# Hybrid decoder block, forgetting attention: VectorE's side jobs issued behind the low parts of a step instead of ahead of them

## The chip, the cores and the metric

One core of a Trainium2 chip runs the whole program. The metric is the device time of one execution in microseconds (us), the median of several runs. Five engines matter: TensorE (PE: matrix products and transposes; PEld: its weight loads), VectorE (DVE), ScalarE (ACT), GpSimd (POOL, next to idle here) and SyncE (SP, which issues all transfers). Each engine works through its own instructions strictly in the order written; they meet at semaphores.

## The reference

One decoder block over 1024 tokens of width 1024, all in float32:

```
h = rms_norm(x);  proj = h @ w_in
qa, ka, va, fa, qb, kb, vb, ga, gb = split(proj)
log_f = log_sigmoid(fa + b_forget);  F = cumsum(log_f)
oa = softmax(qa ka^T / 8 + F_q - F_k, causal) @ va          # "forgetting" attention, 8 heads of 64
ob = mixture over 3 dilated sliding-window attentions        # 12 heads of 64, with rotary embedding
mixed = sigmoid(ga) * (oa @ w_branch_a) + sigmoid(gb) * (ob @ w_branch_b)
x = x + mixed @ w_out
x = x + relu(rms_norm(x) @ w_up)^2 @ w_down
return rms_norm(x)
```

## The kernel before, in words

**Precision.** TensorE is fed with fp32r operands. Every operand is split into a high part (a copy rounded to fp32r, made on ScalarE) and a low part (the rest, `operand - high`, made on VectorE), and a product is three matmuls: high x high, high x low, low x high. So each tensor needs a ScalarE copy and then a VectorE subtraction before TensorE may use it. The subtractions are the "low parts" and "splits" of this text.

**Stages.** The program first norms x, then runs ten attention *units* t = 0 to 9 of two heads each (`mixer_steps`): t = 0 to 5 are the dilated ones (`N_DIL` = 6), t = 6 to 9 the forgetting ones. Then come gates, branch products, output product and the MLP. Four `merge` jobs that sum the three dilated groups are done in the first two steps of t = 6.

**A unit** has 16 steps (G counts steps over all units, s = G mod 16 is the step in its unit). A step is one head and one tile of 128 queries. In a forgetting unit the queries are causal, so a step handles 1, 2, 1, 2, 3, 4, 3, 4, 5, 6, 5, 6, 7, 8, 7, 8 key tiles of 128 for s = 0 to 15. Steps of at least five tiles are worked in two pieces of at most four tiles ("units_of"), which take turns in the two halves of one PSUM tensor.

What the engines do in step G, in this order:

- TensorE: `scores(G)` (L1165), a third of a project part (L1122; the matrix products for the next units' keys, queries and values, which need the weight splits), `transposes(G-1)` of the probabilities (L1176), two more thirds of projection, and in odd steps `values` for an earlier pair of steps (L1197). In step 1 of a unit also the transposes of the values (L1206).
- VectorE: in even steps first `outs` (L2196: adds the two head halves; waits for ScalarE's `o_part`, which waits for TensorE's `values`); then `maxes(G)` (L2175: adds the bias, finds the row maximum; waits for the scores); then the first side job; then `probs_lo(G-1)` (L2182: the low part of the transposed probabilities); in even steps `query_lo` (L2156); in step 1 `values_lo` (L2163); then the other side jobs.
- ScalarE: `exps(G)` (L1627; waits for `maxes(G)`), then `probs_hi(G-1)` (L1637; the high part of the transposed probabilities), then its own splits (L1519, L1599). Before `exps` it has the evacuation of a finished projection (L1559) and `out_part` (L1652).

`transposes(G)` waits for `exps(G)`, and its piece n for the low part of piece n-2, since the pieces share two PSUM halves: in the steps of two pieces that is the low part of the step just before. `scores(G)` waits for `exps(G-2)`.

**Side jobs** of a step are listed by `side_work(G)`. In the forgetting units they are: a half of a weight chunk's low part, `split_lo` (L2077, 128x512; table `LO_STEPS`); a head's key low part, `k_stack` (L2148, 64x1024; table `K_LO_STEPS`); the normalising of the unit before, `normalise` (L2212, 128x1024, step 7); and in the first two steps of t = 6 the four merges (L2206, 128x1024). Nearly every step has one job or none. The steps with jobs are

| unit | split halves | key splits | normalise | merges |
|---|---|---|---|---|
| t = 6 | 2 (two), 6, 7, 13, 14 | 4, 5 | | 0 (two), 1 (two) |
| t = 7 | 3, 4, 9, 10, 14, 15 | 11, 12 | 7 | |
| t = 8 | 5, 6, 12, 13 | 9, 10 | 7 | |
| t = 9 | 3, 4, 10 (two) | | 7 | |

SyncE's loads of later weight chunks wait for the splits too (`w_lo`), with at least a chunk of lead.

Of the kernel before, what the change touches and what calls it, by code (L numbers as in the profile page):

```python
# [53 lines left out]
N_DIL = 2 * len(DILATIONS)  # L54
# [235 lines left out]
def build(nc, x, g_attn, w_in, b_forget, w_branch, w_out, g_mlp, w_up, w_down, g_final, rope, f_rows, r_rows, x_mid, hidden, sg, out):  # L290
# [8 lines left out]
    with ExitStack() as ctx:  # L299
# [1763 lines left out]
        def _(dve):  # L2063
# [19 lines left out]
            for half in range(2):  # L2083
# [7 lines left out]
                for i in range(4):  # L2091
                    t = 4 * half + i
# [58 lines left out]
            def query_lo(B):  # L2151
                t, b = divmod(B, BLOCKS)
                row = 64 * (b % 2)
                cols = slice(b // 2 * 2 * P, (b // 2 + 1) * 2 * P)
                dve.wait_ge(q_hi, 2 * B + 1)
                dve.scalar_tensor_tensor(out=q_st(B)[row:row + 64, 1, :], in0=q_raw(t)[row:row + 64, cols], scalar=-QSCALE,  # L2156
                                         in1=q_st(B)[row:row + 64, 0, :].bitcast(F32),
                                         op0=ALU.mult, op1=ALU.subtract).then_inc(q_lo, 1)

            def values_lo(t):  # L2160
                for bank in range(2):
                    dve.wait_ge(v_hi, 2 * t + bank + 1)
                    dve.tensor_tensor(v_part[1][:, 4 * bank:4 * bank + 4, :, :],  # L2163
                                      PS[2][:, bank * HALF:(bank + 1) * HALF].rearrange("p (t h d) -> p t h d", t=4, h=2),
                                      v_part[0][:, 4 * bank:4 * bank + 4, :, :].bitcast(F32),
                                      ALU.subtract).then_inc(v_lo, 1)

            def maxes(G):
                n = len(tiles_of(G))
                dve.wait_ge(qk_done, G + 1)  # L2170
                if G >= STEPS * N_DIL and G % STEPS == 0:
                    f = G // STEPS - N_DIL
                    dve.wait_ge(fbias_in[f % 2], 32 * (f // 2 + 1))
                sc = psc[G % 2][:, 0:n * P]
                dve.tensor_tensor_reduce(sc, sc, score_bias(G, n), 1.0, FMAX, ALU.add, ALU.min,  # L2175
                                         stat(G, 0)).then_inc(max_done, 1)

            def probs_lo(G):
                for n, (a, b) in enumerate(units_of(G)):
                    u = units_before(G) + n  # L2180
                    dve.wait_ge(pt_hi, u + 1)
                    dve.tensor_tensor(pt_tiles(G, 1, a, b),  # L2182
                                      PS[2][:, (u % 2) * HALF:(u % 2) * HALF + (b - a) * P].rearrange("p (j c) -> p j c", c=P),
                                      pt_tiles(G, 0, a, b).bitcast(F32), ALU.subtract).then_inc(pt_lo, 1)

            def inverses(f):
                dve.wait_ge(exp_done, STEPS * (N_DIL + f + 1))
                cols = slice(f * STEPS, (f + 1) * STEPS)
                dve.reciprocal(rowinv[:, cols], fox_stat[:, 1, cols]).then_inc(inv_done, 1)

            def outs(B):
                t, b = divmod(B, BLOCKS)
                row = 64 * (b % 2)
                dst = og[:, t // 2, (t % 2) * 1024:(t % 2 + 1) * 1024] if t < N_DIL else keep[:, (t - N_DIL) * 1024:(t - N_DIL + 1) * 1024]
                dve.wait_ge(op_done, B + 1)
                dve.tensor_tensor(pair_tokens(dst[row:row + 64], t, b // 2), pair_view(o_bank(B)[row:row + 64, :], t),  # L2196
                                  pair_view(o_part[row:row + 64, :], t), ALU.add).then_inc(on_done, 1)
# [16 lines left out]
            def side_work(G):  # L2214

                t, s = divmod(G, STEPS)
                u = t + 1
                jobs = []
                if t == MIX - 1 and s == 10:
                    jobs += [lambda: split_lo(CH0 + 3 * t + 5, 0), lambda: split_lo(CH0 + 3 * t + 5, 1)]  # L2220
                if t < N_DIL:
                    for s0, s1, c in ((3, 4, 3 * t + 4), (8, 8, 3 * t + 5), (14, 14, 3 * t + 6)):
                        jobs += [lambda c=c: split_lo(CH0 + c, 0)] if s == s0 else []
                        jobs += [lambda c=c: split_lo(CH0 + c, 1)] if s == s1 else []
                    if s in (9, 15):
                        jobs.append(lambda: k_stack(u, (s - 9) // 6))
                elif (t, s) in LO_STEPS:
                    jobs.append(lambda: split_lo(CH0 + LO_STEPS[t, s][0], LO_STEPS[t, s][1]))
                if s in K_LO_STEPS.get(t, ()):
                    jobs.append(lambda: k_stack(u, K_LO_STEPS[t].index(s)))  # L2230
                if t == N_DIL and s in (0, 1):
                    jobs += [lambda: merge(2 * s), lambda: merge(2 * s + 1)]
                if t == N_DIL and s == 2:
                    jobs += [lambda: split_lo(CH0 + 23, 0), lambda: split_lo(CH0 + 23, 1)]
                if t > N_DIL and s == 7:
                    jobs.append(lambda: normalise(t - N_DIL - 1))
                if u < N_DIL:
                    jobs += [lambda n=n: rotate(u, n // 8, n // 4 % 2, n % 4) for n in ROTATE_OPS.get(s, ())]
                return jobs

            def mixer_steps(first, last):
                for G in range(first, last + 3):
                    t, s = divmod(G, STEPS)
                    if G % 2 == 0 and first <= G - 4 < last:
                        outs((G - 4) // 2)
                    jobs = side_work(G) if G < last else []
                    if G < last:
                        maxes(G)
                    for job in jobs[:1]:
                        job()  # L2250
                    if first <= G - 1 < last:
                        probs_lo(G - 1)
                        if first and G > first and s == 0:
                            inverses(t - N_DIL - 1)
                    if G < last and G % 2 == 0 and G // 2 + 1 < BLOCKS * MIX:
                        query_lo(G // 2 + 1)
                    if s == 1 and G < last:
                        values_lo(t)
                    for job in jobs[1:]:
                        job()  # L2260

            for n in range(8):
# [6 lines left out]
            split_lo(4)  # L2269
            query_lo(0)  # L2270
            mixer_steps(0, STEPS * N_DIL)


# [26 lines left out]
            for n in range(6):  # L2300
                g, pair = divmod(n, 2)
                dve.wait_ge(spr_done, n + 1)
                own = og[:, g, pair * 1024:(pair + 1) * 1024]
                dve.tensor_tensor(own, PS[pair][:], own, ALU.mult).then_inc(spr_out, 1)
            mixer_steps(STEPS * N_DIL, STEPS * MIX)


# [528 lines left out]
```

## Time and profile before

| what | value |
|---|---|
| median of 3 runs | 1602.18 us (1600.99 to 1605.12) |
| the profiled execution: own time | 1602.5 us |
| its span in the trace | 1600.7 us |
| PE busy | 1517.0 us (95%), PEld 1243.0 (78%) |
| DVE busy | 1100.1 us (69%) |
| ACT busy | 784.1 us (49%) |
| forgetting units (t = 6 to 9) | about 384.7 to 631 us of the span |

The profiled execution takes 1.8 us more than its span, which lies around the first and last instruction. Starts are in us from the span's start. A group's idle time is that of the engine just before its instructions; behind the arrow stands what ended it. A PE that is busy in this count is not always at its peak, since its matmuls overlap.

### The profile page before, as it was taken

What the parts mean: (1) busy time and instruction counts of PE and PEld (TensorE: products, weight loads), DVE (VectorE), ACT (ScalarE), POOL (GpSimd) and SP (SyncE); (2) the same over time, 40 slices, a digit from 0 to 9 for tenths busy, and PEclk for the clock granted to TensorE, in tenths of its full rate; (3) what the DMA queues carried; (4) which work ended last, traced back from release to release, by engine and by line L of the source; (5) the groups of instructions that cost most, each with busy time, mean ns of one, the idle gap of its engine ahead of it and who ended that gap; (6) DMA issues with size and microseconds to landing.
All of it is one profiled execution on the core that took longest, in us unless ns stands there. A gap on an engine that the chain in (4) does not pass through costs nothing. (4 is left out here: it accounts for less than half of the span.)

```text
span 1600.7 us, 20827 instructions
## 1 busy us (share of the span) xinstructions
PE 1517.0 (95%) x7364; PEld 1243.0 (78%) x7364; DVE 1100.1 (69%) x1749; ACT 784.1 (49%) x1436; POOL 4.8 (0%) x22
## 2 busy tenths in 40 slices
PE   6999999998999998999999989999999899999997
PEld 5787777776777877788888878888888677777776
DVE  4677777755666666943675676766667787777776
ACT  5566666663666665534224454343334444444441
POOL 1000000000000000000000000000000000000000
PEclk9999999999999999999999999999999999999998
DMA  5321111111022111333655333444444774444402
GB/s 184 93 65 29 41 53 41 27 40 27 14 67 65 29 41 34 105 118 100 194 174 152 99 92 124 159 150 161 162 154 169 248 264 145 145 145 145 145 27 106
DMA packets 168277, 173.40 MB, mean 108 GB/s; under 512 B 7848, under 2 KB 127720, under 8 KB 167792
## 3 DMA queue, kind: packets, MB, share of 16 engines
q1 hardware_dynamic: 168176, 172.07, 33.5%
q8 instruction: 61, 1.00, 0.3%
q14 instruction: 40, 0.33, 0.1%
HBM read 125.84 MB, written 46.20 MB: 107 GB/s over the span
## 5 line engine op out<-in xcount | busy, mean ns | idle before, releaser
L1122 PE MATMUL ps<-hspl,wsp 128*128 128x512 f32 x1536 | 423.3, 408 | 8.8 <-ACT tmp L1559 5.1
L1122 PEld LDWEIGHTS ps<-hspl,wsp 128*128 128x128 f32 x1536 | 265.2, 190 | 55.5 <-ACT tmp L1559 7.3
L1474 PE MATMUL ps<-dn_b,a_hi 128*128 128x512 f32 x896 | 279.1, 393 | 17.1 <-DVE keep L2309 11.4
L1474 PEld LDWEIGHTS ps<-dn_b,a_hi 128*128 128x128 f32 x896 | 167.3, 189 | 59.5 <-issue 21.7
L1474 PE MATMUL ps<-dn_b,a_lo 128*128 128x512 f32 x448 | 175.2, 391 | 0.0
L2309 DVE TENSOR_TENSOR keep<-keep,ps 128x512 f32<-128x512 f32 (+1 forms) x144 | 101.4, 712 | 42.7 <-PE ps L1474 24.3
L1474 PE MATMUL ps<-up_b,a_hi 128*128 128x512 f32 x384 | 119.6, 393 | 4.9 <-ACT keep L1908 3.8
L2182 DVE TENSOR_TENSOR work<-ps,work 128x128 fp32r<-128x128 f32 (+3 forms) x144 | 59.1, 420 | 65.8 <-ACT work L1637 63.7
L1932 ACT ACTIVATE keep<-keep 128x512 f32<-128x512 f32 x64 | 40.5, 633 | 126.0 <-DVE keep L2611 42.0
L1474 PEld LDWEIGHTS ps<-dn_b,a_lo 128*128 128x128 f32 x448 | 84.4, 188 | 17.9
L1176 PE MATMUL ps<-ident,tmp 128*128 128x128 f32 x428 | 74.7, 276 | 21.1 <-issue 8.0
L2309 DVE TENSOR_TENSOR dn_b<-dn_raw,dn_b 128x1024 fp32r<-128x1024 f32 x56 | 67.1, 1221 | 39.4 <-ACT dn_b L1948 39.3
L1176 PEld LDWEIGHTS ps<-ident,tmp 128*128 128x128 f32 x428 | 52.1, 140 | 48.8 <-issue 27.0
L2475 DVE TENSOR_TENSOR a_lo<-a_raw,a_hi 128x1024 fp32r<-128x1024 f32 (+1 forms) x66 | 81.3, 1234 | 11.0 <-ACT a_hi L1898 10.9
L1474 PEld LDWEIGHTS ps<-up_b,a_hi 128*128 128x128 f32 x384 | 72.6, 190 | 20.6 <-issue 4.0
L1908 ACT COPY ps<-ps 128x512 f32<-128x512 f32 x46 | 26.3, 571 | 122.6 <-PE ps L1474 115.8
L1627 ACT ACTIVATE tmp<-ps,fox_stat 128x128 f32<-128x128 f32 (+3 forms) x64 | 47.5, 743 | 72.4 <-DVE fox_stat L2175 72.3
L1474 PE MATMUL ps<-up_t,a_hi 128*128 128x512 f32 x256 | 78.9, 389 | 0.0
L1474 PE MATMUL ps<-up_t4b,a_hi 128*128 128x512 f32 x256 | 78.8, 389 | 0.0
L1627 ACT ACTIVATE tmp<-ps,dil_stat 128x128 f32<-128x128 f32 (+1 forms) x96 | 40.1, 417 | 73.8 <-DVE dil_stat L2175 73.6
L1474 PE MATMUL ps<-up_b,a_lo 128*128 128x512 f32 x192 | 75.3, 392 | 0.0
L1197 PEld LDWEIGHTS ps<-work 128*128 128x128 f32 x456 | 68.3, 190 | 7.3 <-DVE work L2182 1.6
(240 smaller groups left out, 2827.1 us busy)
## 6 DMA issues: line engine op xcount, KB each, us to landing
hidden<-keep SPq DMA_DIRECT2D x112, 256.0 KB, 2.2
dn_raw<-hidden SPq DMA_DIRECT2D x56, 512.0 KB, 6.1
raw<-in_w_in SPq DMA_DIRECT2D x35, 512.0 KB, 3.8
a_raw<-in_w_up SPq DMA_DIRECT2D x36, 256.0 KB, 3.1
sgl<-sg SPq DMA_DIRECT2D x8, 1024.0 KB, 5.1
a_raw<-in_w_down SPq DMA_DIRECT2D x32, 256.0 KB, 3.0
spare<-in_w_down SPq DMA_DIRECT2D x32, 256.0 KB, 3.7
spare<-in_w_up SPq DMA_DIRECT2D x28, 256.0 KB, 3.2
```

Of the source, the lines that this page charges most:

```text
L1122: ins = pe.matmul(psp(u, g), wsp[c % 2][:, wp, k * P:(k + 1) * P], hspl[:, mp, k, cols], start=(n == 0), stop=(n == 23), skip_group_check= ...
L1176: ins = pe.transpose(PS[2][:, (u % 2) * HALF + (k - a) * P:(u % 2) * HALF + (k - a + 1) * P], probs(G)[:, k * P:(k + 1) * P], ident[:])
L1197: ins = pe.matmul(o[:, cols], v_nat[:, j, 2 * (b % 2):2 * (b % 2) + 2, :].rearrange("p a d -> p (a d)"), moving, start=(part == 0 and (n = ...
L1474: ins = pe.matmul(o, a_part(n, j, wp, k), b_block(n, j, mp, k), start=(first and k == 0 and m == 0), stop=(k == ks - 1 and m == 2), skip_g ...
L1627: act.activation(probs(G)[:, 0:n * P], psc[G % 2][:, 0:n * P], ACT.Exp, bias=stat(G, 0), scale=-1.0, accum_out=stat(G, 1)).then_inc(exp_do ...
L1908: act.copy(s1[q] if q < 2 else bank_b(q), bank_a(q)).then_inc(s1_ok, 1)
L1932: act.activation(u, u, ACT.Square).then_inc(signal, 1)
L2182: dve.tensor_tensor(pt_tiles(G, 1, a, b), PS[2][:, (u % 2) * HALF:(u % 2) * HALF + (b - a) * P].rearrange("p (j c) -> p j c", c=P), pt_til ...
L2309: return dve.tensor_tensor(out, a, b, op)
L2475: dve.tensor_tensor(a_lo_t[q % 2][b][:], src[:], a_hi_t[q % 2][b][:].bitcast(F32), ALU.subtract).then_inc(a_lo, 1)
```

## The change

In steps of the forgetting units (t at least `N_DIL`) the first side job is no longer issued between `maxes(G)` and `probs_lo(G-1)`; all side jobs are issued behind `probs_lo`, `query_lo` and `values_lo`, at the end of the step. The dilated units stay as they were. No instruction is added, removed or resized; TensorE's, ScalarE's, GpSimd's and SyncE's orders are as before.

```diff
                     jobs = side_work(G) if G < last else []
                     if G < last:
                         maxes(G)
-                    for job in jobs[:1]:
+                    early = 1 if t < N_DIL else 0
+                    for job in jobs[:early]:
                         job()
                     if first <= G - 1 < last:
                         probs_lo(G - 1)
...
                     if s == 1 and G < last:
                         values_lo(t)
-                    for job in jobs[1:]:
+                    for job in jobs[early:]:
                         job()
```

VectorE in t = 6, steps 4 and 5 (L2175: maxes and its accumulator read, L2148: key split, L2182: low part of the probabilities, L2156: query, L2196: outs):

```order
 L2175 ISA ps,fox_stat<-ps,fbias_57 128x384
 L2175 ISA fox_stat 128x1
-L2148 TENSOR_TENSOR work<-tmp,work 64x1024
 L2182 TENSOR_TENSOR work<-ps,pt_odd 128x2x128
 L2156 SCALAR_TENSOR_TENSOR q_fox<-tmp,q_fox 64x256
+L2148 TENSOR_TENSOR work<-tmp,work 64x1024
 L2175 ISA ps,fox_stat<-ps,fbias_57 128x512
 L2175 ISA fox_stat 128x1
-L2148 TENSOR_TENSOR work<-tmp,work 64x1024
 L2182 TENSOR_TENSOR work<-ps,work 128x3x128
+L2148 TENSOR_TENSOR work<-tmp,work 64x1024
 L2196 TENSOR_TENSOR keep<-ps,o_part 64x256
```

Both key splits moved from ahead of the low part to the step's end: that of step 4 now stands directly ahead of the next maxes, that of step 5 ahead of the outs.

VectorE in t = 6, steps 13 and 14 (L2077: half of a weight chunk's split):

```order
-L2077 TENSOR_TENSOR wsp_54<-raw_52,wsp_54 128x512
 L2182 TENSOR_TENSOR work<-ps,work 128x4x128
 L2182 TENSOR_TENSOR work<-ps,work 128x3x128
+L2077 TENSOR_TENSOR wsp_54<-raw_52,wsp_54 128x512
 L2196 TENSOR_TENSOR keep<-ps,o_part 64x256
 L2175 ISA ps,fox_stat<-ps,fbias_57 128x896
 L2175 ISA fox_stat 128x1
-L2077 TENSOR_TENSOR wsp_54<-raw_52,wsp_54 128x512
 L2182 TENSOR_TENSOR work<-ps,work 128x4x128 x2
 L2156 SCALAR_TENSOR_TENSOR q_fox<-tmp,q_fox 64x256
+L2077 TENSOR_TENSOR wsp_54<-raw_52,wsp_54 128x512
```

The split half of step 13 moved behind the two low pieces and stands ahead of outs and the next maxes; that of step 14 moved behind low pieces and query.

## Rows read from the trace of the kernel before

**Rows 1.** The page's busy times of each engine over the span.

```profile
PE 1517.0 (95%) x7364; PEld 1243.0 (78%) x7364; DVE 1100.1 (69%) x1749; ACT 784.1 (49%) x1436; POOL 4.8 (0%) x22
```

**Rows 2.** Groups by line, 384 to 631 us: busy, mean ns, idle before, releaser.

```profile
L1627 ACT ACTIVATE tmp<-ps,fox_stat 128x128 f32<-128x128 f32 (+3 forms) x64 | 47.5, 743 | 72.4 <-DVE fox_stat L2175 72.3
L1176 PE MATMUL ps<-ident,tmp 128*128 128x128 f32 x288 | 43.0, 275 | 11.4 <-DVE work L2182 7.7 <-issue 3.4
L2182 DVE TENSOR_TENSOR work<-ps,pt_odd 128x512 fp32r<-128x512 f32 (+3 forms) x48 | 25.3, 555 | 31.4 <-ACT pt_odd L1637 31.1
...
L2077 DVE TENSOR_TENSOR wsp<-raw,wsp 128x512 fp32r<-128x512 f32 x20 | 13.7, 683 | 0.0
...
L2148 DVE TENSOR_TENSOR work<-tmp,work 64x1024 fp32r<-64x1024 f32 x6 | 7.3, 1220 | 0.2
...
L2212 DVE TENSOR_TENSOR keep<-keep,tmp 128x1024 f32<-128x1024 f32 x3 | 3.7, 1218 | 0.4 <-DMA tmp<-r_rows 0.4
```

**Rows 3.** Timeline: t = 9 step 13; t = 6 step 13 (VectorE); t = 9 steps 10, 11.

```profile
613.42 1.23 DVE L2175 CUSTOM_DVE_ANT_0 ps<-ps,fbias 128x1024 f32<-128x1024 f32 x1
...
614.79 1.12 ACT L1627 ACTIVATE tmp<-ps,fox_stat 128x1024 f32<-128x1024 f32 x1 [2.20 <-DVE fox_stat L2175]
...
615.90 0.96 ACT L1637 CAST work<-ps 128x512 fp32r<-128x512 f32 x2
616.51 1.15 DVE L2182 TENSOR_TENSOR work<-ps,work 128x512 fp32r<-128x512 f32 x2 [1.75 <-ACT work L1637]
...
433.48 0.69 DVE L2077 TENSOR_TENSOR wsp<-raw,wsp 128x512 fp32r<-128x512 f32 x1
435.31 1.16 DVE L2182 TENSOR_TENSOR work<-ps,work 128x512 fp32r<-128x512 f32 x2 [1.15 <-ACT work L1637]
...
604.60 0.68 DVE L2077 TENSOR_TENSOR wsp<-raw,wsp 128x512 fp32r<-128x512 f32 x1
...
605.20 0.95 DVE L2175 CUSTOM_DVE_ANT_0 ps<-ps,fbias 128x768 f32<-128x768 f32 x1
```

**Rows 4.** Timeline, VectorE, t = 6 step 4: key split, then low part.

```profile
399.90 1.22 DVE L2148 TENSOR_TENSOR work<-tmp,work 64x1024 fp32r<-64x1024 f32 x1
401.15 0.42 DVE L2182 TENSOR_TENSOR work<-ps,pt_odd 128x256 fp32r<-128x256 f32 x1
```

**Rows 5.** Waits (us in total, times, longest) in 384:448, 448:507, 507:565, 565:631 in turn.

```profile
DVE keep L2196 <- ACT o_part L1652: 3.9, 3, 1.6
DVE work L2163 <- ACT work L1619: 1.4, 1, 1.4
...
DVE keep L2196 <- ACT o_part L1652: 3.2, 6, 0.8
DVE work L2163 <- ACT work L1619: 2.8, 1, 2.8
...
DVE keep L2196 <- ACT o_part L1652: 3.4, 5, 1.0
...
DVE keep L2196 <- ACT o_part L1652: 1.4, 3, 0.6
DVE work L2163 <- ACT work L1619: 1.6, 1, 1.6
```

**Rows 6.** Timeline, TensorE: waits in t = 6 steps 3 and 15, t = 7 step 15.

```profile
395.88 0.71 PE L1122 MATMUL ps<-hspl,wsp 128*128 128x512 f32 x2 [1.48 <-DVE wsp L2077]
...
440.64 1.05 PE L1176 MATMUL ps<-ident,tmp 128*128 128x128 f32 x7 [0.99 <-DVE work L2182]
...
502.07 1.05 PE L1176 MATMUL ps<-ident,tmp 128*128 128x128 f32 x7 [1.52 <-DVE work L2182]
```

**Rows 7.** Timeline, t = 7: low part of step 12, and the transposes of step 13.

```profile
496.21 1.16 DVE L2182 TENSOR_TENSOR work<-ps,work 128x512 fp32r<-128x512 f32 x2 [1.75 <-ACT work L1637]
...
497.05 1.06 PE L1176 MATMUL ps<-ident,tmp 128*128 128x128 f32 x8
```

## The prediction

> **What bounds the kernel now.** I read the page's busy times first, then the groups and the waits of the forgetting units alone, then the timeline of single steps. Over the span TensorE is the fullest engine at 95%, VectorE has 69% [rows 1]. That average hides what happens in the four units that the change touches. There ScalarE sits idle 72.4 us before its exps, 72.3 of it until VectorE's maxes are done, and VectorE sits idle 31.4 us before the low parts of one buffer (about as long before those of the other), until ScalarE's high parts are done [rows 2]. The two engines feed each other in a ring: maxes(G), exps(G), high part(G-1), low part(G-1), and behind the low part the next maxes. One turn, in t = 9 step 13 [rows 3]: maxes start at 613.42, exps at 614.79, the high part at 615.90, the low part at 616.51, and VectorE has done nothing for 1.75 us before it. TensorE is close behind: its transposes sit idle 7.7 us in all until a low part is done [rows 2], with single waits of 0.99 and 1.52 us late in a unit [rows 6], but it has no such waits in most of the smaller steps. So two chains of nearly equal length run side by side: the ring, and TensorE's own work. Where TensorE is the later one, VectorE waits for it at outs (3.9, 3.2, 3.4 and 1.4 us in the four units) and once a unit at the values' low part (1.4, 2.8, 2.8, 1.6; the row of 2.8 stands for t = 7 and, word for word again, for t = 8) [rows 5].
>
> **What the old place costs.** Nothing in nearly every step. The job stands in the gap in which VectorE waits for ScalarE: with a split half in t = 6 step 13 the job starts at 433.48, and the low part still waits 1.15 us more at 435.31, until the high part [rows 3]. The reader should see that the job only shortens the idle time. A key split of 1.22 us is longer than some gaps of small steps: in t = 6 step 4 the low part follows it with no idle time [rows 4]; a step of that size without so long a job reaches its low part some 1.05 us behind its maxes, so 0.2 us is all the job costs there.
>
> **What the new place costs.** Behind the low part there is no such gap: the next is maxes (after an even step) or outs (after an odd one), and maxes do not wait for TensorE. The ring gets longer by the job, less the idle time that VectorE has at outs. Prices: a split half 0.60 us, from start to start of the next in the one place where a half already stands there (604.60 to 605.20) [rows 3], against a duration of 0.68; a key split 1.25 from start to start [rows 4]; normalise 1.22 [rows 2], of which I count 1.15. The gap itself does not shrink, since ScalarE still needs it, so the job's old time comes back as idle time.
>
> Now unit by unit, as the lag that each unit adds to TensorE, since TensorE's lag is what cannot be taken back at outs:
>
> - t = 6. Step 0 only swaps a merge and the query: 0. Step 1: a merge (128x1024 like normalise, 1.22 long [rows 2], counted 1.14 from start to start) moves behind the values' low part, which gets 0.16 earlier: +0.98. Step 2: a half, +0.60, and TensorE already waits 1.48 us for just this split [rows 6], so 1.58 goes straight to TensorE. Steps 4 to 7: 1.05 + 1.25 + 0.60 + 0.60 = 3.50, less the 1.20 us (one of the three waits that make the 3.9 [rows 5]; the others are 1.55 and 1.11) that VectorE waits at outs of step 6; the 1.55 ahead of step 4 give nothing, as both are late alike. The transposes around step 11 start only 0.2 us behind what they wait for, so TensorE has taken over about 2.1 of these 2.30 by the next outs wait. Step 13: +0.60, less 0.1. Step 14 falls under the values' wait of the next unit (2.8) [rows 5]. Unit: 1.58 + 2.07 + 0.50 = 4.15.
> - t = 7. Steps 3, 4, 9, 10 halves (2.4), 7 normalise (1.15), 11 and 12 key splits (2.5): 6.05 by step 13. Outs waits up to there: 3.2 [rows 5] less the last one of 0.56 = 2.62. Left 3.43, and no time for TensorE to hide it: the transposes of step 13 start at 497.05, and the first piece of the low part of step 12 (0.69 of the 1.16 from 496.21) is done at 496.9 [rows 7], 0.1 earlier; the next ones wait 1.52 us already [rows 6]. Unit: 3.33. Steps 14 and 15 fall under the next values' wait.
> - t = 8. Halves in 5, 6, 12, 13 (2.4), normalise 1.2, key splits in 9 and 10 (2.5): 6.1. Outs waits 3.4 [rows 5] less the 1.03 of step 4, ahead of the first job: 2.37. Unit: 3.73 less 0.1 = 3.6.
> - t = 9. Halves in 3 and 4 (1.2), normalise 0.83 (it waited 0.44 us for a transfer and held the low part up, which is won back), the first half of step 10 (0.6): 2.63. Of the outs waits of 1.4 [rows 5] count 0.59, 0.16 and 0.1 of the third, TensorE being late by then, less 0.1: 1.7.
>
> Sum: 4.15 + 3.33 + 3.6 + 1.7 = **12.8 us**. Dilated units and everything behind t = 9 are unchanged. Loads and the splits themselves end 1 to 4 us later but are wanted a step or more later, except in t = 6 step 3, counted. The profiled execution took 1602.5 us, so 1615.3; it lies 0.3 above the median, so I expect **1615.0 us** as the median.
>
> **Bounds of the unknown.** How much TensorE's own reserve takes up no row tells directly. If nothing absorbed anything, all moved jobs count in full: 6.28 + 7.25 + 6.1 + 2.63 = 22.3 us. If in each unit all of VectorE's waits for TensorE, at outs and at the values, were free for the jobs, the units cost 6.28 - 5.3 = 1.0, 7.25 - 6.0 = 1.25, 6.1 - 6.2 and 2.63 - 3.0, so 0: 2.2 us. I take the middle value since rows 6 and 7 show TensorE with 0.1 us or nothing in hand exactly where the lag has piled up.
>
> **The rivals.**
>
> *TensorE covers it.* TensorE is the bound of a whole unit, and the ring catches up at each values' low part. For it: 95% busy, and 2.8 us of VectorE's waits there in t = 7 and 8 [rows 1, 5]. Against it: TensorE's waits of 0.99 and 1.52 us on low parts late in the unit [rows 6], through which a late ring is handed on before the catching-up point. Time: 1602.2 + 2.2 = 1604.4. Beside this stands the Trainium skill, "Perfetto Trace Analysis", section "Identifying the Most-Contended Engine": the engine with the highest occupancy is the most contended and the one to work on. By that rule an order on an engine of 69% would be worth nothing while TensorE stands at 95%, and the time would be 1602.2; the waits between engines speak against it here.
>
> *Full exposure.* The outs waits do not absorb, because TensorE gets late at once. For it: transposes follow exps closely in some steps. Against it: in early steps TensorE shows no waits at all. Time: 1602.2 + 22.3 = 1624.5.
>
> *Faster.* The low parts come earlier, so TensorE's transposes stop waiting. It decides if the jobs, and not ScalarE, release the low parts. The price is the 7.7 us of TensorE's waits on low parts [rows 2]: 1594.5. Against it: VectorE is idle before nearly all low parts, with a job or without [rows 3]; the low part that is held up is held by 0.2 us [rows 4]. Without that mechanism what is left of it is under 1 us.
>
> *Another thing than told:* the moved jobs could make a step's scores or loads late. All have a step or more in hand; it would add to the forecast, not replace it.
>
> **How the numbers follow.** A difference under 0.3% (4.8 us) counts as no change here. My forecast (12.8, with 8 to 18 as its own range) gets 0.70, TensorE covering it (up to 4.8) 0.16, full exposure 0.11, faster 0.03. Slower by over 4.8 us holds the first and third: 0.81; no change 0.16; faster 0.03. The range of 8 in 10 leaves out the coverer and the far end of full exposure: 1607 to 1622.
>
> **What would show it.** In the changed profile: no side job between maxes and low part in t = 6 to 9; idle time before low parts up by about the 20 us of the moved jobs (31.4 and its twin, together some 62, towards 80); each of the units t = 6 to 8 longer by 3 to 4 us, t = 9 by 2; VectorE's waits at outs smaller than in rows 5; more TensorE idle before transposes, by about 10 us over the 7.7. The units before t = 6 and all after t = 9 the same length. I am wrong if the four units together grow by under 5 us (TensorE had reserve), or if the idle time before the low parts does not grow (the jobs were not hidden before).

## The result and the profile after

| | kernel before | changed kernel |
|---|---|---|
| median | 1601.59 us (1600.80 to 1605.12, 4 runs) | 1620.23 us (1618.33 to 1620.52, 4 runs) |
| the profiled execution: span | 1600.7 us | 1616.5 us |
| 0 to the first maxes of t = 6 | 384.7 us | 384.7 us |
| from there to the last maxes of t = 9 | 237.5 us | 253.6 us |

The ratio of the medians is 1.0100, 95% interval [1.0084, 1.0116]: the change costs 1.0%, by the medians 18.6 us, by the profiled executions 15.8 us. The units themselves grow by 16.1 us; the 2.5 us more of the medians have no place in the two traces, where all that stands behind the last maxes took 978.5 and 978.2 us. Over the twelve traces of this text that last part took 977.6 to 984.5 us, so medians and spans carry a few us that the units do not explain, and the growth of the units is the sharper instrument here.

The page's busy times stand beside [rows 1]:

```profile
PE 1520.8 (94%) x7364; PEld 1244.5 (77%) x7364; DVE 1099.7 (68%) x1749; ACT 783.9 (48%) x1436; POOL 4.8 (0%) x22
```

VectorE and ScalarE did the same work in the same time. Only TensorE's busy time grew, by 3.8 us (2.6 of them in the four units), which the order of another engine's jobs should not do; about 1.6 of these 2.6 us are a slow clock, taken up below. Where the time lies the busy times by stretch tell (us; then busy time and instructions of PE, PEld, DVE, ACT and POOL; granted clock, DMA share, GB/s):

```profile
0.00:384.00 384.00, 355.03 (x1876) 288.66 (x1877) 262.65 (x629) 228.16 (x579) 4.83 (x22) 1.00 0.20 61
384.00:647.00 263.00, 229.81 (x1353) 187.04 (x1353) 159.02 (x332) 154.61 (x361) 0.00 (x0) 0.99 0.12 35
647.00:1616.00 969.00, 935.95 (x4137) 768.84 (x4136) 678.08 (x789) 401.13 (x496) 0.00 (x0) 0.99 0.44 145
```

The same work took 247 us before (384 to 631), and the rest is as long as it was. All of the loss is in the four forgetting units. The groups there, to hold against [rows 2]:

```profile
L1122 PE MATMUL ps<-hspl,wsp 128*128 128x512 f32 x456 | 137.1, 420 | 13.0 <-ACT tmp L1559 9.7 <-DVE wsp L2077 3.2
L1627 ACT ACTIVATE tmp<-ps,fox_stat 128x128 f32<-128x128 f32 (+3 forms) x64 | 47.5, 742 | 89.2 <-DVE fox_stat L2175 89.1
L1176 PE MATMUL ps<-ident,tmp 128*128 128x128 f32 x288 | 43.3, 276 | 17.3 <-DVE work L2182 12.8 <-issue 3.4 <-ACT tmp L1627 0.9
L2182 DVE TENSOR_TENSOR work<-ps,pt_odd 128x512 fp32r<-128x512 f32 (+3 forms) x48 | 25.3, 555 | 42.1 <-ACT pt_odd L1637 42.1
L2182 DVE TENSOR_TENSOR work<-ps,work 128x512 fp32r<-128x512 f32 (+3 forms) x48 | 25.3, 555 | 41.5 <-ACT work L1637 41.5
```

- ScalarE waits 89.1 us for maxes instead of 72.3: +16.8, about the whole loss. The maxes come late, and with them the exps.
- VectorE waits 83.6 us in front of the low parts instead of some 62: +22. The jobs that filled the gap are gone from it, and the gap is as long as before.
- TensorE waits 12.8 us for low parts at its transposes (7.7 before), 3.2 for a weight split (1.5 before) and 9.7 for ScalarE's evacuation of a finished projection. That last one was 3.9 in the kernel before, a row I had not read.

The waits of VectorE at outs in the four units (384 to 451, 451 to 515, 515 to 579, 579 to 647 us), and the one at the values' low part that changed, in t = 8, to hold against [rows 5]:

```profile
DVE keep L2196 <- ACT o_part L1652: 4.2, 2, 3.1
...
DVE keep L2196 <- ACT o_part L1652: 1.1, 3, 0.6
...
DVE keep L2196 <- ACT o_part L1652: 1.2, 2, 1.0
DVE work L2163 <- ACT work L1619: 2.4, 1, 2.4
...
DVE keep L2196 <- ACT o_part L1652: 0.8, 2, 0.6
```

The outs waits fell in t = 7 to 9 (3.2, 3.4, 1.4 before), as forecast, and did not fall in t = 6. There one single wait of 3.07 us stands at step 4:

```profile
402.11 0.42 DVE L2196 TENSOR_TENSOR keep<-ps,o_part 64x256 f32<-64x256 f32 x1 [3.07 <-ACT o_part L1652]
```

It was 1.55 before, of the 3.9 of [rows 5]; the wait of 1.20 at step 6 is gone, taken up by late jobs as forecast. Something slowed TensorE between 394 and 402 us. The wait for the weight split is part of it; the rest is the clock, as the next timeline shows. It is TensorE from step 3 of t = 6 on, first after, then before:

```profile
397.54 0.71 PE L1122 MATMUL ps<-hspl,wsp 128*128 128x512 f32 x2 [3.21 <-DVE wsp L2077]
...
398.12 2.80 PE L1122 MATMUL ps<-hspl,wsp 128*128 128x512 f32 x6
400.72 0.95 PE L1197 MATMUL ps<-work 128*128 128x256 f32 x4
```

```profile
396.45 1.62 PE L1122 MATMUL ps<-hspl,wsp 128*128 128x512 f32 x6
397.91 0.57 PE L1197 MATMUL ps<-work 128*128 128x256 f32 x4
```

The same six matmuls take 2.80 us instead of 1.62, and the next four 0.95 instead of 0.57. The granted clock of these microseconds (the eighth figure, behind POOL's) is full before the wait and half behind it:

```profile
398.00:399.00 1.00, 1.00 (x5) 0.73 (x3) 0.25 (x1) 0.95 (x4) 0.00 (x0) 0.62 0.39 58
399.00:400.00 1.00, 1.00 (x4) 0.80 (x3) 0.04 (x1) 0.65 (x1) 0.00 (x0) 0.50 1.03 300
400.00:401.00 1.00, 1.00 (x5) 0.81 (x4) 0.00 (x0) 0.00 (x0) 0.00 (x0) 0.50 0.56 166
401.00:402.00 1.00, 1.00 (x7) 0.84 (x7) 0.00 (x0) 0.29 (x1) 0.00 (x0) 0.67 0.00 0
402.00:403.00 1.00, 1.00 (x7) 0.84 (x7) 0.89 (x3) 0.49 (x2) 0.00 (x0) 1.00 0.00 0
```

In the kernel before, the clock is 1.00 all through this stretch. So TensorE ran at 1.2 GHz in place of 2.4 for some 3 us, right behind a wait of 3.21 us. From the two matmul groups it costs (2.80 - 1.62) + (0.95 - 0.57) = 1.56 us.

### The profile page after: what moved, and what is told of

Same layout as the page of the kernel before. It is cut to its first block and busy times, and to the rows that moved or that the text cites. A ratio compares the mean times of both kernels' runs of the same rounds, so it can differ in the third digit from the quotient of the medians.

```text
span 1616.5 us, 20827 instructions
## 1 busy us (share of the span) xinstructions
PE 1520.8 (94%) x7364; PEld 1244.5 (77%) x7364; DVE 1099.7 (68%) x1749; ACT 783.9 (48%) x1436; POOL 4.8 (0%) x22
## 5 line engine op out<-in xcount | busy, mean ns | idle before, releaser
L1474 PE MATMUL ps<-dn_b,a_hi 128*128 128x512 f32 x896 | 279.8, 394 | 16.6 <-DVE keep L2310 12.1
L1474 PEld LDWEIGHTS ps<-dn_b,a_hi 128*128 128x128 f32 x896 | 167.5, 189 | 59.1 <-issue 22.8
L1474 PE MATMUL ps<-dn_b,a_lo 128*128 128x512 f32 x448 | 175.5, 392 | 0.0
L1474 PE MATMUL ps<-up_b,a_hi 128*128 128x512 f32 x384 | 120.2, 395 | 4.8 <-ACT keep L1908 3.8
L2182 DVE TENSOR_TENSOR work<-ps,work 128x128 fp32r<-128x128 f32 (+3 forms) x144 | 59.1, 420 | 76.9 <-ACT work L1637 74.7
L1176 PE MATMUL ps<-ident,tmp 128*128 128x128 f32 x428 | 74.9, 276 | 27.1 <-DVE work L2182 12.8
L1474 PEld LDWEIGHTS ps<-dn_b,a_lo 128*128 128x128 f32 x448 | 84.8, 189 | 17.9
L1627 ACT ACTIVATE tmp<-ps,fox_stat 128x128 f32<-128x128 f32 (+3 forms) x64 | 47.5, 742 | 89.2 <-DVE fox_stat L2175 89.1
L1474 PEld LDWEIGHTS ps<-up_b,a_hi 128*128 128x128 f32 x384 | 73.0, 191 | 20.6 <-issue 4.0
L1474 PE MATMUL ps<-up_t4b,a_hi 128*128 128x512 f32 x256 | 79.5, 392 | 0.0
L1474 PE MATMUL ps<-up_t,a_hi 128*128 128x512 f32 x256 | 78.9, 389 | 0.0
L1474 PE MATMUL ps<-up_b,a_lo 128*128 128x512 f32 x192 | 75.6, 394 | 0.0
L1197 PEld LDWEIGHTS ps<-work 128*128 128x128 f32 x456 | 68.7, 191 | 7.4 <-DVE work L2182 1.6
```

The source lines that it names most:

```text
L1176: ins = pe.transpose(PS[2][:, (u % 2) * HALF + (k - a) * P:(u % 2) * HALF + (k - a + 1) * P], probs(G)[:, k * P:(k + 1) * P], ident[:])
L1197: ins = pe.matmul(o[:, cols], v_nat[:, j, 2 * (b % 2):2 * (b % 2) + 2, :].rearrange("p a d -> p (a d)"), moving, start=(part == 0 and (n = ...
L1474: ins = pe.matmul(o, a_part(n, j, wp, k), b_block(n, j, mp, k), start=(first and k == 0 and m == 0), stop=(k == ks - 1 and m == 2), skip_g ...
L1627: act.activation(probs(G)[:, 0:n * P], psc[G % 2][:, 0:n * P], ACT.Exp, bias=stat(G, 0), scale=-1.0, accum_out=stat(G, 1)).then_inc(exp_do ...
L2182: dve.tensor_tensor(pt_tiles(G, 1, a, b), PS[2][:, (u % 2) * HALF:(u % 2) * HALF + (b - a) * P].rearrange("p (j c) -> p j c", c=P), pt_til ...
```

## Where the lag comes in

I matched all 64 maxes of the units in the two traces and read the difference of their starts. How much each unit grows, in us (from the first maxes of t = 6 to those of t = 7 step 0, t = 8 step 2, t = 9 step 2 and t = 9 step 15), for the changed kernel and for the experiments below:

| kernel | t = 6 | t = 7 | t = 8 | t = 9 | sum |
|---|---|---|---|---|---|
| forecast | 4.15 | 3.33 | 3.6 | 1.7 | 12.8 |
| changed kernel | 6.4 | 4.0 | 3.6 | 2.1 | 16.1 |
| e1_not_first | 3.2 | 4.0 | 3.6 | 2.8 | 13.6 |
| e2_first_only | 2.9 | 0.0 | 0.0 | 0.2 | 3.1 |
| e3_odd_only | 2.2 | 1.2 | 1.2 | 0.7 | 5.3 |
| e4_even_only | 2.7 | 1.9 | 1.5 | 3.1 | 9.3 |
| h1_extra_early | 0.0 | 0.0 | 0.0 | 0.2 | 0.2 |
| h3_extra_late | 2.4 | 0.7 | 1.3 | 0.6 | 5.0 |
| f1_query_early | -2.1 | -0.9 | -0.9 | -1.5 | -5.4 |
| f3_query_outs_early | -3.4 | -1.8 | -1.4 | -3.9 | -10.4 |
| f4_order_late | 1.2 | 0.2 | -0.5 | -2.7 | -1.7 |

From here on "units" with a number means the last column. Each row is one traced execution. The spans grow by up to 6.3 us more than these sums (in f1; 4.9 in e3, 4.0 in f4, about 2 or less in the others): up to 1.2 us of that lies before t = 6 and the rest behind t = 9. The step of one split half is 0.58 to 0.61 us, very regular, in every step in which nothing takes it back.

## The experiments

### One part of the change at a time

The first two cut the change at the start of t = 6. e1 leaves steps 0 to 2 of t = 6 as they were, and e2 changes these three alone. The edit of e1:

```diff
-                    early = 1 if t < N_DIL else 0
+                    early = 1 if t < N_DIL or G < STEPS * N_DIL + 3 else 0
```

> Jobs moved as in the change except in steps 0 to 2 of t = 6, which stay as in the kernel before. Theory A (the moved jobs lengthen the ring of VectorE and ScalarE; VectorE's waits at outs absorb part): the span grows by 11 to 13 us over the kernel before, and the granted clock stays at full speed around 398 us. Theory B (every moved job costs in full, nothing absorbs): 21 us. Theory C (the loss is mostly the clock that fell after TensorE's long wait for the first split): only some 5 us.

Measured: 1616.08 us (1614.99 to 1616.77) against 1602.09, ratio 1.0088 [1.0074, 1.0101]; units +13.6, a little above the 11 to 13 expected. Some 0.7 us of it is one more wait, of 0.87 us, in which the normalise of t = 9, now at the step's end, waits for its transfer (0.15 us in the changed kernel). TensorE's wait for the split is 1.5 us again, and the clock stays full:

```profile
396.00:399.00 3.00, 2.07 (x10) 1.69 (x11) 1.48 (x5) 2.07 (x5) 0.00 (x0) 1.00 0.32 74
399.00:402.00 3.00, 3.00 (x19) 2.46 (x18) 1.01 (x4) 1.82 (x7) 0.00 (x0) 1.00 0.33 101
```

The edit of e2:

```diff
-                    early = 1 if t < N_DIL else 0
+                    early = 0 if STEPS * N_DIL <= G < STEPS * N_DIL + 3 else 1
```

> Only steps 0 to 2 of t = 6 changed (two merges and one split half moved). Theory A: the ring is 1.6 us late at maxes of step 3, TensorE's wait for the split grows from 1.5 to 3.2 us, the granted clock falls behind it as in the changed kernel and adds 1.5: 3.1 us in all, kept to the end. Rival (the clock's fall has another cause, such as a transfer at that time): 1.6 us and full clock. Theory C: 10 us or more.

Measured: 1605.01 us (1604.12 to 1607.66), ratio 1.0019 [1.0010, 1.0029]; units +3.1, of which t = 6 has 2.9. The wait and the slow clock are there with these three steps alone:

```profile
PE ps L1122 <- DVE wsp L2077: 3.2, 1, 3.2
```

```profile
400.00:401.00 1.00, 1.00 (x4) 0.81 (x3) 0.00 (x0) 0.33 (x1) 0.00 (x0) 0.50 1.13 343
401.00:402.00 1.00, 1.00 (x6) 0.91 (x6) 0.00 (x0) 0.00 (x0) 0.00 (x0) 0.50 0.18 52
402.00:403.00 1.00, 1.00 (x5) 0.66 (x5) 0.50 (x2) 0.79 (x2) 0.00 (x0) 0.65 0.00 0
```

So the first three steps cost their 1.6 us of late jobs and about 1.3 us of clock more, as expected, and everything else of the change costs 13.6 without the clock. 3.1 + 13.6 = 16.7, against the 16.1 of the whole; the rest is e1's longer wait for the transfer.

The expectation of e2 names a rival for the clock, a transfer at that time. There is one: DMA share 1.03 to 1.13 in the slow microseconds. But the same burst stands at full clock in other traces, as here in e4, where TensorE's wait for the split is 2.1 us:

```profile
399.00:400.00 1.00, 1.00 (x8) 0.85 (x7) 0.00 (x0) 0.46 (x2) 0.00 (x0) 1.00 1.14 346
```

So the transfer alone does not do it.

The next two cut it by kind of step. After an odd step an outs stands behind the moved job and may take it in; after an even one the maxes stand there. e3 moves the jobs of odd steps alone, e4 those of even steps alone. The edit of e3 (e4 has `s % 2 == 0`):

```diff
-                    early = 1 if t < N_DIL else 0
+                    early = 0 if t >= N_DIL and s % 2 else 1
```

> Jobs moved in odd steps alone (there outs, which waits for TensorE in many steps, stands behind the job). Theory A: 13.3 us of jobs are moved, the outs waits absorb more than half: some 5 us. Theory B: 13 us.

Measured: 1610.00 us (1609.07 to 1612.66), ratio 1.0054 [1.0042, 1.0067]; units +5.3, as expected. The median is up by 7.9; in the trace 1.0 us more lies before the units and 3.8 behind them.

> Jobs moved in even steps alone (there the next maxes stand behind the job, which wait for nothing but VectorE). Theory A: 8.6 to 9.8 us of jobs are moved; the next outs waits still absorb part, so some 5 us, and no fall of the clock. Theory B: 9 us. If odd and even together give much less than the change (under 11 against 16), the waits at outs are a reserve that is used up: each half alone fits into it, both together do not.

Measured: 1612.31 us (1610.26 to 1615.09), ratio 1.0068 [1.0055, 1.0081]; units +9.3. That is a miss, about 4 us over. Two of them come in at one place, t = 9 step 8, with the normalise job. It stands early in e4, as in the kernel before, and waits for its transfer:

```profile
600.35 1.23 DVE L2212 TENSOR_TENSOR keep<-keep,tmp 128x1024 f32<-128x1024 f32 x1 [2.45 <-DMA tmp<-r_rows]
```

It waited 0.44 us before. The transfer's load was issued at 595.47, behind the store of the inverse rows at 591.84 and a weight load at 591.43, in the order of SyncE's queue; before, the same three came at 586.45, 582.91 and 582.50, some 9 us earlier, while the maxes of step 7 lie only 7.4 us later than before. By the code the weight load waits for a split, which stands later in its step here, and the store stands behind that load in the queue; that this is the reason was not tried by itself. A job in the gap costs nothing only as long as what it waits for has come. In the whole change the normalise stands at the step's end and 0.15 us of this wait are left.

With the prices of the prediction the jobs of odd steps are 12.9 us long in all (t = 6: 3.6, t = 7: 4.2, t = 8: 3.65, t = 9: 1.4) and those of even steps 9.5. So 5.3 of 12.9 us show in odd steps, 41%, and 9.3 - 2.0 = 7.3 of 9.5 in even ones, 77%: the outs behind an odd step do take in a good part, and a job straight ahead of the maxes shows for the most part. The two halves without the 2 us sum to 12.6, the whole change without its clock to 16.1 - 1.5 = 14.6; so some 2 us of reserve are shared between them, far from the case (under 11 against 16) in which the expectation would have seen a reserve used up.

### Is the gap free, and is the end of the step what costs

The change moves 29 jobs of three sizes. A cleaner test adds one: a subtraction of 128x512 elements that writes to unused scratch memory and leaves the output as it is, in the 16 steps whose only split job is one half (the table's split halves without step 2 of t = 6 and step 10 of t = 9, which have two). h1 puts it in the gap, right behind the first side job, so that the gap must hold two:

```diff
+            def filler():
+
+                dve.wait_ge(dchain, chain[0])
+                chain[0] += 1
+                dve.tensor_tensor(stage5[:, :], hspl[:, 0, 0, 0:HALF].bitcast(F32), hspl[:, 1, 0, 0:HALF].bitcast(F32),
+                                  ALU.subtract).then_inc(dchain, 1)
...
                     for job in jobs[:1]:
                         job()
+                    if G < last and (t, s) in LO_STEPS:
+                        filler()
```

> The kernel before with one more subtraction of the size of a split half (128x512, read from SBUF, written to a scratch) in each of the 16 steps of LO_STEPS, in the gap between maxes and low part. Theory A (the gap is ScalarE's time and free for VectorE): the gap left there is 0.45 to 1.2 us against 0.6 us of work, so the four units grow by under 1 us. Rival (any work on VectorE costs, wherever it stands): 16 x 0.6 = 10 us.

Measured: 1602.95 us (1599.63 to 1605.99) against 1603.31, ratio 1.0000 [0.9990, 1.0010]; units +0.2 for 16 x 0.6 = 9.6 us of new work. The maxes of t = 7 step 0, t = 8 step 0 and t = 9 step 7 lie 1.14, 1.12 and 1.16 us behind those of the kernel before, and the first maxes of t = 6, ahead of all fillers, already 1.13. t = 6 step 13 on VectorE, to hold against the second part of [rows 3] (L2182 is the maxes' line in this kernel, L2189 that of the low part):

```profile
434.62 0.69 DVE L2077 TENSOR_TENSOR wsp<-raw,wsp 128x512 fp32r<-128x512 f32 x1
435.23 0.69 DVE L2172 TENSOR_TENSOR stage<-hspl 128x512 f32<-128x512 f32 x1
436.46 0.69 DVE L2189 TENSOR_TENSOR work<-ps,work 128x512 fp32r<-128x512 f32 x1 [0.55 <-ACT work L1637]
```

The low part comes 1.84 us behind the split, as before (433.48 to 435.31: 1.83), and its wait fell from 1.15 to 0.55. h3 has the same filler, behind `for job in jobs[1:]` at the step's end:

```diff
                     for job in jobs[1:]:
                         job()
+                    if G < last and (t, s) in LO_STEPS:
+                        filler()
```

> The same 16 additional subtractions, but at the end of their steps; the real jobs stay in the gap. Theory A: the units grow by what the change showed for the same steps, step by step together some 6.4 us (0.6 in most even steps, 0 in those odd steps that stand before a long wait at outs). If it is as little as in the run with the work in the gap, the place is not what costs.

Measured: 1608.51 us (1604.09 to 1612.22), ratio 1.0037 [1.0026, 1.0047]; units +5.0, so half of the 9.6 us, where some 6.4 were expected. The groups of h1, then of h3, in the four units:

```profile
L1627 ACT ACTIVATE tmp<-ps,fox_stat 128x128 f32<-128x128 f32 (+3 forms) x64 | 47.5, 742 | 72.8 <-DVE fox_stat L2182 72.7
L2203 DVE TENSOR_TENSOR keep<-ps,o_part 64x256 f32<-64x256 f32 x31 | 13.1, 421 | 12.4 <-ACT o_part L1652 11.7
```

```profile
L1627 ACT ACTIVATE tmp<-ps,fox_stat 128x128 f32<-128x128 f32 (+3 forms) x64 | 47.5, 743 | 79.3 <-DVE fox_stat L2182 79.2
L2203 DVE TENSOR_TENSOR keep<-ps,o_part 64x256 f32<-64x256 f32 x31 | 13.1, 421 | 9.2 <-ACT o_part L1652 8.6
```

In the gap the filler changes neither row (72.3 and 11.8 us in the kernel before); what it takes is VectorE's idle time before the low parts, 61.5 us before, 52.1 in h1 and again 61.5 in h3. At the step's end it lets ScalarE wait 6.5 us more for maxes. In VectorE's time, h3 against h1, the 9.6 us are 4.8 of longer units, 3.1 less of outs waits, 0.4 less at the values' low part and 0.7 less at the normalise's transfer; 0.6 stay unplaced.

### Turning it round: more work into the gap

If the ring bounds these units, whatever leaves its path should win time. In the forgetting units f1 puts the query's low part, which stood between the low part and the next maxes, ahead of the low part, into the gap:

```diff
+                    if t >= N_DIL and G < last and G % 2 == 0 and G // 2 + 1 < BLOCKS * MIX:
+                        query_lo(G // 2 + 1)
                     if first <= G - 1 < last:
                         probs_lo(G - 1)
...
-                    if G < last and G % 2 == 0 and G // 2 + 1 < BLOCKS * MIX:
+                    if t < N_DIL and G < last and G % 2 == 0 and G // 2 + 1 < BLOCKS * MIX:
                         query_lo(G // 2 + 1)
```

> The kernel before, with query_lo in the forgetting units ahead of the low part of the probabilities instead of behind it. Theory A read the other way round: 0.35 to 0.45 us leave the ring in each even step, where TensorE is not the bound: the units shrink by 1 to 4 us. Rival (TensorE's own work bounds the units): no change.

Measured: 1598.74 us (1595.57 to 1603.43) against 1603.31, ratio 0.9972 [0.9963, 0.9982]; units -5.4, more than the 1 to 4 expected. f3 has this edit and one more: outs no longer stands ahead of the maxes but behind them.

```diff
-                    if G % 2 == 0 and first <= G - 4 < last:
+                    if (not first or G >= last) and G % 2 == 0 and first <= G - 4 < last:
                         outs((G - 4) // 2)
                     jobs = side_work(G) if G < last else []
                     if G < last:
                         maxes(G)
+                    if first and G < last and G % 2 == 0 and first <= G - 4:
+                        outs((G - 4) // 2)
```

> As before, and outs also behind maxes, in the gap, instead of ahead of maxes, so that VectorE's wait for TensorE's values falls into the gap. Theory A: ring shorter by some 0.8 us in each even step; TensorE's waits on low parts (7.7 us) and on evacuations (3.9 us) are the most that can be won: 3 to 8 us faster. Rival: no change.

Measured: 1593.61 us (1591.88 to 1594.23), ratio 0.9942 [0.9930, 0.9954]; units -10.4, more than the 3 to 8 expected. This is faster than both kernels. Its groups in the units:

```profile
L1627 ACT ACTIVATE tmp<-ps,fox_stat 128x128 f32<-128x128 f32 (+3 forms) x64 | 47.5, 742 | 53.9 <-DVE fox_stat L2175 53.2
L1176 PE MATMUL ps<-ident,tmp 128*128 128x128 f32 x288 | 42.9, 275 | 5.2 <-issue 3.4 <-DVE work L2182 1.6
L2175 DVE CUSTOM_DVE_ANT_0 ps<-ps,fbias 128x128 f32<-128x128 f32 (+3 forms) x64 | 48.7, 762 | 20.2 <-PE ps L1165 19.8
```

ScalarE's waits for maxes fell by 19 us, and TensorE hardly waits for low parts now. The third row is new: VectorE waits 19.8 us for TensorE's scores in front of the maxes (1.2 us of idle time in all before). The ring has overtaken TensorE in many steps and TensorE is what bounds there.

### Both together

f4 is f3 with the change on top, f5 the kernel of f3 once more as its partner on the same chip.

> Query and outs early, as in f3_query_outs_early, and the change with it: the first side job of each step of t = 6 to 9 behind the low part. Theory A (the jobs cost because they lengthen the ring of VectorE and ScalarE, whatever else stands in it): the ring is shorter by the query and by the outs now, but the gap in front of the low part has no more idle time to give, and no outs wait is left that could take a job in. So the step from f3 to f4 should be no smaller than the 15.8 us of the change itself, up to the 22 us of all jobs in full where the ring is what bounds, and less by what the shorter ring leaves as TensorE's lead. I expect units t = 6 to 9 longer by 12 to 18 us than those of f3, so 1606 to 1612 us. Theory B (the gap is what costs, and a ring shortened by the new order has room for the jobs at its end): under 6 us more than f3, so below 1600.

> The kernel of f3_query_outs_early once more, on the same chip as f4, as its partner. Both theories: 8 to 10 us faster than the kernel before, ratio 0.994 to 0.995, as the first time.

Measured: f5 1593.11 us (1591.41 to 1593.87), ratio 0.9943 [0.9929, 0.9956], as the first time. f4 1602.79 us (1599.97 to 1605.86), ratio 1.0006 [0.9996, 1.0015]. So late jobs cost 9.7 us on this order by the medians, in the units 10.4 - 1.7 = 8.7 us, some 1.4 of them in the step of the slow clock again. Neither theory's figure came out: it is less than the 12 us or more that A asked for and more than the 6 that B allowed. The rows of f4 say why:

```profile
L2175 DVE CUSTOM_DVE_ANT_0 ps<-ps,fbias 128x128 f32<-128x128 f32 (+3 forms) x64 | 48.7, 761 | 11.7 <-PE ps L1165 11.2
L2182 DVE TENSOR_TENSOR work<-ps,pt_odd 128x512 fp32r<-128x512 f32 (+3 forms) x48 | 25.3, 555 | 31.3 <-ACT pt_odd L1637 31.3
```

Of f3's 19.8 us of waits for scores, 11.2 are left; 8.6 us of late jobs went into them for nothing. VectorE's waits for ScalarE before the low parts rose from 41.2 to 60.0 us, by 18.8 and not by the 22 us of all moved jobs, so part of the jobs seems to have cost time already in f3's fuller gap. I had written that the gap had nothing more to give and had overlooked that the ring itself now had reserve. By unit the change costs 4.6, 2.0, 0.9 and 1.1 here, in t = 8 a quarter of the 3.6 that it costs in the order before. What the change costs depends on which of the two chains is the later one, and by how much.

## Why the prediction was right, and where its sum was off

The median is 1620.2 us, forecast 1615.0 in 1607 to 1622, and the case that I held likeliest is the one that came. It lies 5.2 us over the forecast and near the upper end of the range: 3.3 us are misses in the units, taken apart below, and the rest is the few us of the medians that no trace places. That the range held them all is partly luck, since it had no term for the clock. By its own steps:

- **The gap is free, the step's end is not.** Right, and shown: 9.6 us of new work in the gap cost 0.2 us in the units (h1), at the step's end 5.0 (h3). Idle time before the low parts rose from 62 to 83.6 us, forecast "towards 80".
- **The prices.** A split half 0.60 from start to start: measured 0.58 to 0.61 in a dozen steps. Right.
- **The middle of the units.** Up to t = 6 step 13 the forecast has 1.58 + 2.07 us, measured are 1.54 (steps 2 and 3) and 2.07 (steps 5 to 8), apart from what step 4 brings. Up to t = 7 step 14: 3.40, forecast 3.33. t = 8: 3.6, forecast 3.6. t = 9: 2.1, forecast 1.7, its normalise step having brought 0.97 instead of 0.83. Right.
- **t = 6 step 4, missing.** "1.58 goes straight to TensorE" was right, and made TensorE's wait of [rows 6] 3.21 instead of 1.48 us; I did not ask what a wait of that length does to TensorE's clock. It fell to half, and the lag grew by 1.53 us in this one step. e1 (without them) and e2 (with them alone) show that it belongs to the first three steps; why the clock fell behind this wait is not shown (last section).
- **The last half of a unit, the step of the sum that was wrong.** "Step 14 falls under the values' wait of the next unit", and the same of steps 14 and 15 of t = 7. It did not: t = 6 grew by 0.58 and 0.59 in steps 14 and 15, where 0.50 in all was forecast, and nothing came back in t = 7; t = 7 grew by another 0.6 net. The values' wait of t = 7 is 2.8 us as before, that of t = 8 fell only to 2.4. TensorE had become as late by then. I had looked only at its transposes; it also waits for ScalarE's evacuation of a projection (L1559), and ScalarE does that in order, behind exps that are late with the maxes. In t = 7 step 0 the lag of the last half crosses over there, whole; TensorE before, then after:

```profile
445.26 0.73 PE L1122 MATMUL ps<-hspl,wsp 128*128 128x512 f32 x2 [0.50 <-ACT tmp L1559]
```

```profile
451.68 0.73 PE L1122 MATMUL ps<-hspl,wsp 128*128 128x512 f32 x2 [1.11 <-ACT tmp L1559]
```

The wait grew by 0.61 us, one half. The miss of 16.1 - 12.8 = 3.3 us is thus 1.5 of clock, 0.6 + 0.6 of last halves, 0.4 in t = 9 and 0.2 of small differences.

- **"More TensorE idle before transposes, by about 10 us":** it was 5.1 us on low parts, 5.8 on evacuations and 1.7 on the split. The size was near, the place was half wrong.
- **"Nothing absorbs" as a rival, 22.3 us:** not so here, 16.1, and 14.6 without the clock. **TensorE covers it, 2.2 us:** not so here either, though f3 and f4 show that it is no idle thought: once the ring is shortened by 10 us, TensorE covers 8.6 us of the same jobs. Beside this rival stood the Trainium skill ("Perfetto Trace Analysis", section "Identifying the Most-Contended Engine"): work first on the engine with the highest occupancy. The same section warns that TensorE's matmul busy share is no good measure of how close it is to its peak, and names its weight-load share among those to use; that is 78% here, still above VectorE's 69%. That VectorE's order would be worth nothing by it was the prediction's own conclusion, which the section does not draw, and the runs contradict it: this order cost 1.0% when made worse and won 0.6% when made better. In the four units alone TensorE's share is 227.2 of 247 us, 92%, no clearer.

## What to carry to other kernels

Where two engines hand work back and forth, what stands in the gap in which one waits for the other costs nothing (here 0.2 of 9.6 us), and what stands between its last answer and its next question costs up to its full length (here 5.0 of 9.6 us), however low the engine's busy share. So before touching such an order, list per turn what lies on the path from one answer to the next question, and move all that nobody waits for into the gap, up to the gap's length and as long as its own inputs have come; here the query and the outs won 0.6%. The price of a late job is its length less the lead that the other chain has, so cost it anew on every order, and look at all instructions by which the ring's engines serve the bound engine, not only the best known one.

## What the runs showed of the hardware

TensorE's clock can be halved for a few microseconds in the middle of a dense kernel. At this place, in the same few microseconds of the program, TensorE's waits for the split were 1.2 us in f3, 1.5 in the kernel before and in e1, 2.1 in e4, 2.6 in e3, 2.9 in f4 and 3.2 in e2 and the changed kernel. The granted clock stayed at 1.00 in the first five and fell to 0.50 for about 3 us in the last three, here each time only after the wait was over, and cost about 1.3 to 1.5 us. The row of f4:

```profile
400.00:401.00 1.00, 1.00 (x3) 0.72 (x3) 0.00 (x0) 0.50 (x1) 0.00 (x0) 0.50 1.08 321
```

The Trainium skill ("TensorE: Matmul & The Clock Gate", section "What's actually happening") says that the array's own activity sets the gate and that there is a full rate and a half rate, nothing between. The rows agree on the two rates: 1.00 and 0.50, with a value between them (0.62, 0.67) only in the microseconds in which it changes.

The length of one wait does not decide alone, however. Two other places stand in all twelve traces with waits that hardly differ. Before its last values (L1197, behind the last maxes of t = 9) TensorE waits 1.56 us each time; the clock fell in three executions (e3, f1, f4) and stayed at 1.00 in nine. Before a product of the MLP (L1474) it waits 3.83 or 3.84 us; the clock fell during that wait or just behind it in eleven, and stayed at 1.00 in f3. Here is f1 at the first place, where the clock fell behind the short wait:

```profile
623.63 0.53 PE L1197 MATMUL ps<-pt_odd,work 128*128 128x256 f32 x1 [1.56 <-DVE work L2182]
...
624.00:625.00 1.00, 1.00 (x6) 1.00 (x6) 0.00 (x0) 0.00 (x0) 0.00 (x0) 0.50 0.00 0
```

And f3 at the second, where it stayed up behind the long one:

```profile
946.76 0.70 PE L1474 MATMUL ps<-up_b,a_hi 128*128 128x512 f32 x2 [3.83 <-ACT keep L1908]
...
947.70:948.70 1.00, 1.00 (x6) 0.78 (x6) 0.98 (x2) 0.35 (x1) 0.00 (x0) 1.00 0.79 225
```

So these runs give no length of wait from which on the clock falls, and with one traced execution of each kernel they do not show that the changed kernel loses this time in every execution. What else decides was not tried. A forecast should ask of every lengthened wait of TensorE whether the clock may fall behind it, and give that a price and a chance of its own: where it did, a wait that grew from 1.5 to 3.2 us cost about 3.2 us, not 1.7.
